# A two-layer transformer block on one Trainium2 core: output products that end tile by tile, a turned narrow product, index queries for three tiles, scores between transposes, and high parts made with one input

## What is computed

```python
# layer 1
y = concatenate([y_a, y_b, y_c]) * silu(z)
x = x + rms_norm(y @ w_out, post_norm_g)
# layer 2
h = rmsnorm(x, attn_norm)
q, k, v, iq, ik, iw, z, xbc, dt_raw, gate_a, gate_b = split(h @ w_in)
rel = relu(einsum('bqhd,bsd->bqhs', iq, ik) * IDX_DIM ** -0.5)      # 8 index heads of 64
score = einsum('bqhs,bqh->bqs', rel, iw * IDX_HEADS ** -0.5)
top_s, sel = top_k(where(admissible, score, -inf), 128)
o = softmax(q . k[sel]) @ v[sel]                                    # 16 heads, 4 of keys
merged = sigmoid(gate_a) * (o @ w_attn_branch) + sigmoid(gate_b) * (y_ssd @ w_ssd_branch)
x = x + merged @ w_out
x = x + hier_moe(rmsnorm(x, ffn_norm), ...)
```

## Time and profile before

| what | value |
|---|---|
| median of three runs | 1577.42 us (1576.61 to 1577.51) |
| the profiled execution, its own time | 1578.34 us |
| its span in the trace | 1576.5 us |
| PE busy | 1368.4 us (87%) |
| POOL busy | 827.3 us (52%) |
| DVE, ACT busy | 635.3 us, 378.2 us |
| mean granted clock of TensorE | 0.941 |

### The profile page before, as it was taken

One profiled execution on the slowest core, in us unless ns is written; L12 is line 12 of the kernel. 1 busy time (PEld: TensorE's weight loads), 2 busy tenths in 40 slices (PEclk: granted clock), 3 DMA queues, 4 the chain that ended last, 5 costly groups with the idle time before them and its releaser, 6 DMA issues.

```text
span 1576.5 us, 18167 instructions
## 1 busy us (share of the span) xinstructions
PE 1368.4 (87%) x7076; PEld 984.2 (62%) x7076; DVE 635.3 (40%) x929; ACT 378.2 (24%) x736; POOL 827.3 (52%) x712
## 2 busy tenths in 40 slices
PE   5898969589987978999999999968998499999993
PEld 5777747477766745678777878857877333333331
DVE  3131252324887056364877556463221411111112
ACT  3211053311130156311122544251003011111111
POOL 7678713537677710288888333749690213333320
PEclk9999989799999989999999999979997599999997
DMA  5423210132122210023222211352255079999964
GB/s 191 136 67 107 67 41 28 38 107 94 67 81 98 90 53 2 14 94 133 80 87 71 71 41 68 128 232 80 80 220 207 13 314 376 372 373 376 368 246 177
DMA packets 85237, 216.29 MB, mean 137 GB/s; under 512 B 23509, under 2 KB 32421, under 8 KB 71589
## 3 DMA queue, kind: packets, MB, share of 16 engines
q1 hardware_dynamic: 62076, 199.22, 33.7%
q0 software_dynamic: 13824, 8.44, 1.8%
q10 hardware_dynamic: 9256, 7.51, 1.5%
HBM read 255.99 MB, written 26.22 MB: 179 GB/s over the span
## 4 chain that ended last, share of the span: by engine, by line
PE 44%; issue 11%; POOL 11%; PEld 10%; DVE 9%; DMA 4%; DVEq 3%; ACT 3%; POOLq 3%; PEldq 2%; ACTq 1%; SPq 0%
PE ps L963 9%; PE ps L133 6%; PE ps L134 6%; PE ps L135 6%; POOL w_lo L487 6%; PE ps L975 5%; POOL w_hi L484 5%; PEld ps L133 4%; PEld ps L134 3%; PEld ps L135 3%; POOLq L485 2%; PE ps L734 2%; PE ps L955 2%; PE ps L822 1%; DMA w_gu<-w_up,over_u 1%
## 5 line engine op out<-in xcount | busy, mean ns | idle before, releaser
L484 POOL TENSOR_TENSOR w_hi<-stage,unit 128x512 fp32r<-128x512 f32 (+2 forms) x304 | 323.8, 1096 | 444.0 <-PE ps L135 434.3
L487 POOL TENSOR_TENSOR w_lo<-stage,w_hi 128x512 fp32r<-128x512 f32 (+2 forms) x304 | 404.7, 1362 | 10.8
L133 PE MATMUL ps<-hi,w_hi 128*128 128x512 f32 (+1 forms) x600 | 240.3, 401 | 31.8 <-POOL w_lo L487 17.9
L134 PE MATMUL ps<-hi,w_lo 128*128 128x512 f32 (+1 forms) x600 | 237.0, 395 | 0.0
L135 PE MATMUL ps<-lo,w_hi 128*128 128x512 f32 (+1 forms) x600 | 236.8, 395 | 0.0
L133 PE MATMUL ps<-w_hi,hi 128*128 128x512 f32 (+3 forms) x560 | 199.2, 356 | 12.6 <-POOL w_lo L487 6.6
L134 PE MATMUL ps<-w_hi,lo 128*128 128x512 f32 (+3 forms) x560 | 197.0, 352 | 0.0
L135 PE MATMUL ps<-w_lo,hi 128*128 128x512 f32 (+3 forms) x560 | 196.9, 352 | 0.0
L963 PE MATMUL ps<-w_gu,xT 128*64 128x512 f32 x768 | 172.0, 600 | 3.2 <-DMA w_gu<-w_up,over_u 1.8
L133 PEld LDWEIGHTS ps<-hi,w_hi 128*128 128x128 f32 x600 | 116.5, 194 | 63.1 <-issue 19.3
L135 PEld LDWEIGHTS ps<-lo,w_hi 128*128 128x128 f32 x600 | 116.4, 194 | 24.0
(11 more groups left out here) (393 smaller groups left out, 1714.7 us busy)
## 6 DMA issues: line engine op xcount, KB each, us to landing
stage<-w_in SPq DMA_DIRECT2D x84, 512.0 KB, 4.2
w_gu<-w_gate SPq DMA_DIRECT2D x32, 1024.0 KB, 11.6
w_gu<-w_up SPq DMA_DIRECT2D x32, 1024.0 KB, 13.7
...
```

What stands on the lines that cost most here:

```text
L133: pe.matmul(out, x[0], w[0], start=first, stop=False)
L134: pe.matmul(out, x[1], w[0], start=False, stop=False)
L484: nc.gpsimd.tensor_tensor(w_hi[:, b, k, 0:n], stage[:, b, k, 0:n], unit[:].broadcast_to([P, n]), ALU.mult)
L487: last = nc.gpsimd.tensor_tensor(w_lo[:, b, k, 0:n], stage[:, b, k, 0:n], w_hi[:, b, k, 0:n].bitcast(F32), ALU.subtract)
```

## The change

1. **High parts.** POOL makes `w_hi` with `tensor_scalar` times 1.0, not with `tensor_tensor` and a broadcast column of ones. Its loops are written out, and the clearing of `xg` also waits for the last use of the weights.
2. **Output products by tile.** Job 8's and job 37's product is `tokens_by_tile`: eight blocks of a tile and a half, in an order that ends tile 0 at the fourth block, tile 1 at the fifth, tile 2 at the seventh and tile 3 at the eighth. It waits for both halves of the weights ahead of its first matmul. The norm behind it goes by tile, and `turn_tiles` turns all eight chunks of a tile at once into both PSUM sets.
3. **Narrow product.** The 104-column job comes ahead of the index queries (in SP's loads and POOL's splits too), with the weights stationary: 24 matmuls of 512 columns, where 96 of 104 stood. ACT copies the result to `small`, and four transposes bring it back behind the index queries' product.
4. **Index path.** Product, rotation and transposes of the index queries are made for tiles 1 to 3. The scores of tile 1 put eight heads in one PSUM set.
5. **Attention.** The first scores are issued ahead of the loop, the scores of batch i+1 between the two halves of the transposes of batch i-1. Job 14's product moves into the second attention: four eighths, the first scores, four eighths. DVE waits `t_full` before it overwrites `pr`. `gate_next` is read out in step 0 of ACT's loop, from another buffer.

```diff
...
-halves(w2, 0, IQ2)
 for h in range(2):
     rows = slice(512 * h, 512 * (h + 1))
     a = w2[rows, IK2:IK2 + 72].rearrange("(k p) n -> p k n", p=P)
     b = w2[rows, DT2:DT2 + 32].rearrange("(k p) n -> p k n", p=P)
     tile(lambda t, a=a, b=b: [(t[:, :, 0:72], a), (t[:, :, 72:SMALL], b)])
+halves(w2, 0, IQ2)
 for c0 in (KV2, Q2, Q2 + 512, GA2, GB2, GA2 + 512, GB2 + 512, XBC2 + 2048):
...
     for k in range(HALF):
-        nc.gpsimd.tensor_tensor(w_hi[:, b, k, 0:n], stage[:, b, k, 0:n], unit[:].broadcast_to([P, n]), ALU.mult)
+        nc.gpsimd.tensor_scalar(w_hi[:, b, k, 0:n], stage[:, b, k, 0:n], 1.0, None, ALU.mult)
...
-split_job(JOB_SMALL, SMALL)
-with pool.Fori(JOB_SMALL + 1, JOB_Z) as i:
-    split_job(i)
-with pool.Fori(JOB_Z, JOB_Z + 4) as i:
-    split_job(i, 256)
-with pool.Fori(JOB_Z + 4, JOBS) as i:
-    split_job(i)
+narrow = {JOB_MQ: 256, JOB_SMALL: SMALL, **{JOB_Z + i: 256 for i in range(4)}}
+for i in range(1, JOBS):
+    split_job(i, narrow.get(i, 512))
...
+pool.wait_ge(w_used, 2 * JOBS)
...
+def tokens_by_tile():
+    s = turns.take()
+    both = (weights(), weights())
+    for t, half in ((0, 0), (1, 0), (2, 0), (0, 1), (1, 1), (3, 0), (2, 1), (3, 1)):
+        for k in range(HALF):
+            last = matmul3(pe, ps[s][:, t, :], parts(x_parts, everything, HALF * half + k, slice(P * t, P * (t + 1))),
+                           parts(w_parts, everything, both[half], k, slice(0, 512)),
+                           half == 0 and k == 0, half == 1 and k == HALF - 1)
+        if (t, half) == (3, 0):
+            last.then_inc(w_used, 1)
+        if half == 1:
+            last = pe.drain().then_inc(wo_tile, 1)
+            if t == 3:
+                pe.drain().then_inc(w_used, 1)
+    pe.drain().then_inc(turn_full, 1)
...
-    for c0 in (0, 4):
-        s = turns.take()
-        for t in range(TT):
-            pe.wait_ge(tile_rows, base + t + 1)
+    sets = (turns.take(), turns.take())
+    for t in range(TT):
+        pe.wait_ge(tile_rows, base + t + 1)
+        for c0, s in zip((0, 4), sets):
             for c in range(4):
                 last = pe.transpose(ps[s][:, c, P * t:P * (t + 1)], rows(t, c0 + c), ident[:])
-        last.then_inc(turn_full, 1)
+            if t == TT - 1:
+                last.then_inc(turn_full, 1)
...
+    chunks = first() if first else iter(())
+    for _ in range(4 if first else 0):
+        next(chunks)
     turns.settle(1)
+    scores(0, p_s).then_inc(s_full, 1)
+    for _ in chunks:
+        pass
     for i in range(batches + 2):
         if i == 1:
             turns.settle(0)
-        if i < batches:
-            if base + i > 0:
-                pe.wait_ge(s_free, base + i)
-            scores(i, p_s).then_inc(s_full, 1)
-        elif beside:
+        if i == 0:
+            pe.wait_ge(s_free, base + 1)
+            scores(1, p_s).then_inc(s_full, 1)
+        if i >= batches and beside:
             if i == batches:
...
                 if half == 0:
                     pe.wait_ge(exp_ready, base + b + 1)
+                elif i + 1 < batches:
+                    pe.wait_ge(s_free, base + i + 1)
+                    scores(i + 1, p_s).then_inc(s_full, 1)
                 if base + b + half > 0:
                     pe.wait_ge(pT_ready[1 - half], base + b + half)
...
 tokens(ready=6)
+tokens_by_tile()
+turn_tiles(lambda t, c: qt[:, t, P * c:P * (c + 1)], 0)
+s = turns.take()
+for half in range(2):
+    pe.wait_ge(lo_ready, 7 + half)
+    b = weights()
+    for k in range(HALF):
+        last = matmul3(pe, ps[s][0:SMALL, 0, :], parts(w_parts, everything, b, k, slice(0, SMALL)),
+                       parts(x_parts, everything, HALF * half + k, everything), half == 0 and k == 0, half == 1 and k == HALF - 1)
+    last.then_inc(w_used, 1)
+pe.drain().then_inc(turn_full, 1)
+tokens(tiles=range(1, TT))
+pe.wait_ge(small_turned, 1)
+s = turns.take()
+for t in range(TT):
+    last = pe.transpose(ps[s][:, t, 0:SMALL], small[:, P * t:P * (t + 1)], ident[0:SMALL, 0:SMALL])
+last.then_inc(turn_full, 1)
 tokens()
-turn_tiles(lambda t, c: qt[:, t, P * c:P * (c + 1)], 0)
-tokens(ready=8)
-tokens(n=SMALL)
-tokens()
 pe.wait_ge(iq_rows, 1)
-turn_rows(lambda t, c: iqt[:, t, P * c:P * (c + 1)], chunks=4)
+turn_rows(lambda t, c: iqt[:, t, P * c:P * (c + 1)], tiles=range(1, TT), chunks=4)
...
 for n in range(1, TT):
-    for h4 in range(2):
+    for h4 in range(1 if n == 1 else 2):
         s = turns.take()
-        for h in range(4):
+        for h in range(8 if n == 1 else 4):
...
-            last = pe.matmul(ps[s][:, h, 0:P * (n + 1)], iqT[lanes, i // 2, P * n:P * (n + 1)],
+            place = ps[s][:, 2 * (h % 2) + h // 4, 256 * (h // 2 % 2):256 * (h // 2 % 2 + 1)] if n == 1 else ps[s][:, h, 0:P * (n + 1)]
+            last = pe.matmul(place, iqT[lanes, i // 2, P * n:P * (n + 1)],
...
 turn_rows(lambda t, c: qt[:, t, P * c:P * (c + 1)])
-features()
...
+attention(16, scores2, values2, lambda b: query_block(b) + 1, lambda b: pr2[:, b % 2], lambda b: pT2, 8, feature_chunks, feature_chunks)
 pe.wait_ge(yah_ready, 16)
 pe.wait_ge(yal_ready, 16)
...
 tokens(ready=14)
-tokens()
+tokens_by_tile()
...
+    A.activation(qt[:, t, :], xres[:, t, :], ACT.Copy, scale=st[:, 2, 12 + t:13 + t]).then_inc(tile_rows, 1)
+for t in range(TT):
+    A.wait_ge(wo_tile, t + 1)
+    A.activation(yT[:, 0, :], ps[s][:, t, :], ACT.Square, accum_out=st[:, 0, 20 + t:21 + t])
+    A.drain().then_inc(wo_ready, 1)
+    A.wait_ge(ss_ready, t + 1)
+    A.activation(st[:, 1, 8 + t:9 + t], st[:, 0, 8 + t:9 + t], ACT.Sqrt, scale=1.0 / D, bias=st[:, 9, 0:1]).then_inc(post_root, 1)
+    if t > 0:
+        row_out(t - 1)
+    A.wait_ge(tile_ready, t + 1)
+    A.activation(junk, xres[:, t, :], ACT.Square, accum_out=st[:, 0, 12 + t:13 + t])
+    A.drain()
+    A.activation(st[:, 1, 12 + t:13 + t], st[:, 0, 12 + t:13 + t], ACT.Sqrt, scale=1.0 / D, bias=st[:, 9, 0:1]).then_inc(root_ready, 1)
+turns.skip()
+row_out(TT - 1)
 high_parts("attn")
 s = turns.see()
-A.activation(iqt[:], ps[s][:], ACT.Copy).then_inc(iq_ready, 1)
+A.activation(small[:], ps[s][0:SMALL, 0, :], ACT.Copy).then_inc(small_turned, 1)
+A.drain().then_inc(turn_free[s], 1)
+s = turns.see()
...
+A.activation(iqt[:, 1:TT], ps[s][:, 1:TT], ACT.Copy).then_inc(iq_ready, 1)
 A.drain().then_inc(turn_free[s], 1)
 s = turns.see()
...
         A.wait_ge(rel_used, i - 1)
-    A.activation(rel[i % 2][:, :, 0:P * (n + 1)], ps[s][:, :, 0:P * (n + 1)], ACT.Relu).then_inc(rel_ready, 1)
+    if i == 0:
+        A.activation(rel[0][:], ps[s][:], ACT.Relu).then_inc(rel_ready, 1)
+    else:
+        A.activation(rel[i % 2][:, :, 0:w], ps[s][:, :, 0:w], ACT.Relu).then_inc(rel_ready, 1)
     A.drain().then_inc(turn_free[s], 1)
-    if i in (1, 3):
+    if i in (0, 2):
         s = turns.see()
-        A.activation(qt[:, :, 256 * (i - 1):256 * (i - 1) + 512], ps[s][:], ACT.Copy).then_inc(q_ready, 1)
...
-A.drain().then_inc(turn_free[s], 1)
-A.dma_start(gates_dram[1], gate_next[:]).then_inc(gate_saved[1], 16)
 for i in range(16 + 2):
     if i < 16:
         softmax(i, 8, P * (query_block(i) + 1), pr2[:, i % 2], pr2[:, i % 2], False)
-    if i == 1:
-        A.wait_ge(gate_saved[1], 16)
+    if i == 0:
+        s = turns.see()
+        A.activation(gate_next[:], ps[s][:], ACT.Tanh, scale=0.5)
+        A.drain().then_inc(turn_free[s], 1)
+        A.dma_start(gates_dram[1], gate_next[:]).then_inc(gate_saved[1], 16)
     if 0 <= i - 1 < 16:
...
+            if i > 1:
+                V.wait_ge(t_full, 2 * i - 2)
...
-V.wait_ge(wo_ready, 2)
-s = turns.see()
-V.tensor_tensor(st[:, 0, 8:8 + TT], st[:, 0, 8:8 + TT], st[:, 0, 20:20 + TT], ALU.add).then_inc(ss_ready, 1)
-V.wait_ge(rms_ready, 4)
-V.reciprocal(st[:, 2, 8:8 + TT], st[:, 1, 8:8 + TT])
-V.drain()
+s = turns.next_set()
...
+    V.wait_ge(wo_ready, 2 + t)
+    V.tensor_tensor(st[:, 0, 8 + t:9 + t], st[:, 0, 8 + t:9 + t], st[:, 0, 20 + t:21 + t], ALU.add).then_inc(ss_ready, 1)
+    V.wait_ge(post_root, t + 1)
+    V.reciprocal(r, st[:, 1, 8 + t:9 + t])
+    V.drain()
     V.scalar_tensor_tensor(xn[:, t, 0:512], xn[:, t, 0:512], r, post_g[:, 0:512], ALU.mult, ALU.mult)
     V.scalar_tensor_tensor(xn[:, t, 512:D], ps[s][:, t, :], r, post_g[:, 512:D], ALU.mult, ALU.mult)
     V.drain()
     V.tensor_tensor(xres[:, t, :], xres[:, t, :], xn[:, t, :], ALU.add).then_inc(tile_ready, 1)
-    if t > 0:
-        recip(t - 1, 12, 0)
+    recip(t, 12, 0)
+turns.see()
 V.drain().then_inc(turn_free[s], 1)
-recip(TT - 1, 12, 0)
...
         V.wait_ge(s_full, 8 + i + 1)
+        if i > 1:
+            V.wait_ge(t_full, 2 * (8 + i) - 2)
         for h in range(4):
             V.tensor_tensor_reduce(pr2[:, i % 2, h, 0:width], p_s[:, h, 0:width], sel[:, n, 0:width],
...
-    if i == 1:
+    if i == 3:
         V.wait_ge(gate_saved[1], 16)
...
-s = turns.see()
+s = turns.next_set()
 for t in range(TT):
+    V.wait_ge(wo_tile, TT + t + 1)
     V.tensor_tensor(xres[:, t, 512:D], xres[:, t, 512:D], ps[s][:, t, :], ALU.add).then_inc(tile_ready, 1)
```

(10 more changed lines are left out.)

91 lines of the change are left out of this document (42 added, 49 removed).

## The result

| what | before | after |
|---|---|---|
| median | 1577.01 us (4 runs, 1575.06 to 1577.51) | 1589.05 us (4 runs, 1588.35 to 1589.79) |
| ratio to before | | 1.0079, 95% interval 1.0061 to 1.0096 |
| profiled execution, span | 1578.34, 1576.5 us | 1588.35, 1586.5 us |

The change makes the kernel 12 us slower. The forecast was 1536 with a range of 1515 to 1566: wrong, on the wrong side. It came out where rival (b) stands, to which I had given one chance in ten.

A forecast was written before the change was run, and what follows sets the result against it. PE, busy 87% of the span, was taken as the bound. The terms 18.7 + 6.5 - 4.3 + 7.9 + 0.75 - 2.8 + 18.9 - 4.2 = 41.5 us came off 1578.3, giving a median of 1536, range 1515 to 1566.

The forecast's parts named there:

- rival (b): POOL's splits: new high part slower than the low part's two-input form, gain gone from 1.27 us, 1590 at 1.43; chance 0.10.
- the price of the high part: POOL's time for one new high-part instruction, 0.74 to 0.76 us taken, between 0.47 and 1.01; old form 1.01.
- g: Time saved per half split on POOL: 1.0 us forecast, 2.1 at 0.47 us per high part, 0 at 1.01.
- First attention: First scores ahead of the loop, window batches' scores between transposes: 6.5 us gained, nothing in the memory batches.
- Layer 1's tail: Layer 1's output product by tile: 10.45 us lost by starting later, 6.1 gained behind it, net -4.3.
- Layer 2's tail: Output product at job 37 by tile: the same 10.45 us lost, 6.2 gained before routing, net -4.2.
- Narrow product and index queries: Fewer matmuls in both products and no wait ahead of keys and values, less new waits: net +7.9 us.
- Second attention: Scores between transposes and job 14's product around the first scores: +18.9 us, less 2.8 waiting for q's evacuation.
- The steady part: Second attention's steps: scores cover the wait for DVE's copy, 0.8 us in each of 12 batches with three widths, 9.6.
- The splits: PE's waits for POOL's half splits, from program start to behind `xtok`, shrink: 18.7 us gained at 1.0 us per half.
- the wait for both halves: Ahead of each output product's first matmul: start 8.3 us later, 1.65 for slower clock, some 0.5 for drains, 10.45 lost.
- Rival (d): Output products: waiting for both halves costs more than the tails return, 12.3 us more lost, 1549; chance 0.05.

The follow-up runs named there:

- e1: The changed kernel with the high part made by the old two-input broadcast form again; 1573.53 us, ratio 0.9961.
- e3: The changed kernel with the high part made by a converting copy; 1533.21 us, ratio 0.9721.
- e7: The kernel before with the high part made by a converting copy and POOL's loops written out; 1552.62 us, ratio 0.9871.
- e2: The kernel before with the one-input constant high part alone and POOL's loops written out; 1594.69 us, ratio 1.0103.
- e5: e3's kernel with the wait for the second half of the weights moved ahead of the fourth block in both output products; 1509.62 us, ratio 0.9595.
- e11: e5's kernel with both output products signalling their four tiles only after the last matmul; 1529.28 us, ratio 0.9691.
- e9: e5's kernel with job 14's product ahead of the second attention, as before the change; 1518.40 us, ratio 0.9622.
- e12: e5's kernel with the waits for turned keys and queries behind the first four eighths of job 14's product; 1507.90 us, ratio 0.9560.
- e6: e1's kernel with the wait for the second half of the weights moved ahead of the fourth block in both output products; 1549.42 us, ratio 0.9827.

## Why the prediction was wrong

**The step that failed is the price of the high part.** I bounded the new instruction by 0.47 us (from a clearing) and by 1.26 (the dearer of the old forms), took 0.75, and drew the sum from it. It measured 1.46, outside both ends, so g was -1.8 and not 1.0. The upper end had no reason that excluded more: rows 3 and 4 show no arithmetic with a constant on POOL, and "reads one input less" is not a duration. Rival (b) said that from 1.27 us on the gain is gone and that 1.43 gives 1590; the chip gave 1.46 and 1589. Its mechanism was right (a split as long as half a product, and longer waits ahead of jobs 8 and 37), its chance of 0.10 was too small for a price that no row showed. That its number fits to a microsecond is partly luck, as the next paragraph shows. The Trainium skill's figure (GPSIMD Engine Reference, § 3.1: 769 ns for 512 elements) agreed with my middle, and no form measured here has it.

**The price is not all of it.** Of the 53 us between 1536 and 1589, 36.5 are the price: 21 that the sum counted on for g = 1.0, and 15.5 that the dearer form costs (e1 to after). The other 16.5 are the order of the change, which is worth 4 us at g = 0 (e1) where the sum had 20. Rival (b) had both wrong, and they cancel: it went from 1557 up by 33 us, the chip from 1573.5 by 15.5.

**The price is not linear, as I had it.** I gave 20 us to every 0.25. From 0.57 to 1.01 (e3 to e1) it is 40 us, 23 to each 0.25; from 1.01 to 1.46 (e1 to after) 15.5 us, 8.6. By the ratios it is 38 and 19 us. In the old order the two steps are worth 23 us (e7) and 17 (e2). On the slow side something is given back, in what POOL does to DVE. The first taps of the convolution, POOL and DVE, in the kernel after:

```profile
782.64 6.32 POOL L489 TENSOR_SCALAR w_hi<-stage 128x512 fp32r<-128x512 f32 x4
783.86 2.92 DVE L1723 TENSOR_SCALAR xsT<-cpad,cols 128x512 f32<-128x512 f32 x4 [8.15 <-ACT cpad L1264]
```

In e3:

```profile
722.80 2.29 POOL L489 CAST w_hi<-stage 128x512 fp32r<-128x512 f32 x4 [1.76 <-PE ps L139]
725.24 5.58 POOL L492 TENSOR_TENSOR w_lo<-stage,w_hi 128x512 fp32r<-128x512 f32 x4
724.67 5.01 DVE L1723 TENSOR_SCALAR xsT<-cpad,cols 128x512 f32<-128x512 f32 x4 [8.54 <-ACT cpad L1264]
```

Such a tap takes 796 ns in the mean after, all of it beside the constant form. It takes 1233 in e1 and 1312 in e3, but there it lies mostly beside the two-input low part and not beside the high part. What each form does by itself is told by single taps of the second kind (`xsT<-cpad,cols,xsT`, L1727, L1730 in e1) that lie beside one form from start to end:

| POOL's form | its own time beside nothing | the tap beside it | run, start of the tap |
|---|---|---|---|
| none | | 0.74 us | e3, 731.96 |
| copy | 0.61 us | 1.09 us | e3, 735.79 |
| constant | 1.49 us | 1.09 us | after, 771.10 |
| two inputs, one broadcast | 1.04 us | 1.52 us | e1, 764.10 |
| two inputs | 1.26 us | 1.77 us | e3, 740.53 |

Over all such taps beside one form the means are 1.01 us (copy, e3), 0.92 (constant, after), 1.42 (broadcast, e1) and 1.67 (two inputs, e1). In the single taps of the table three forms hold a tap up by their own time less some 0.25 us. The constant form, the longest, holds it up by no more than the copy does. DVE is busy 40 us less after than before, and the convolution stage is no longer after (197.7 us) than in e1 (198.9), though POOL's halves are 1.8 us longer. That the shorter taps are what keeps the stage from growing is argued from these rows, not shown by a run. The rule of the Trainium skill that I cited (SBUF — State Buffer, "Who interferes with whom") speaks of who waits for whom by ports, and of an exclusive lock. A lock held for nearly all of POOL's instruction fits three of the forms, and not the constant form; that the form changes DVE's time this much the page does not say.

**Point by point, with the wrong price taken out** (e1 against before, where g = 0):

- First attention: forecast 6.5 gained, measured 7.2. Right; the memory batches keep a period of 4.7 us.
- Layer 1's tail: forecast at g = 0 a loss of 9.3 + 2.15, measured 9.1 + 3.3; forecast a gain of 6.1, measured 4.9 (6.6 after). The mechanism is right. What stands behind the wait was too small: the drains inside the product take 1.2 us (e5 against e11) and not 0.5, and the clock 2.1 (e1 against e5) and not the 1.65 that I took from shorter waits.
- Layer 2's tail: the same loss, measured 10.2 + 4.0 (the wait itself is 9.39); the gain of 6.2 was 4.9. But routing, which I had left out, took 3.0 us more. With the losses the term is -12.3 where I had -5.2, the largest miss but for the price.
- Narrow product and index queries: forecast 7.9 at g = 1, measured 4.0 at g = 0 and 6.5 at g = 1.75. The stall for the split ahead of the index queries was foreseen at 4 to 5 us; it is 8.2 after, 6.3 in e1 and 4.6 in e3. The narrow product was foreseen at 5.5 to 5.9 us and takes 8.50 in e1 and e3, with a clock of 0.50 for its first 3.75 us (e3). In e5, behind the same wait of 3.2 us, the clock is 1.00 and it takes 5.89; what makes that difference no run shows.
- Second attention: forecast 16.1, measured 12.2 in e1 and 14.3 in e3. The steady part was foreseen at 9.6 and is 9.6 (e9, with the first scores ahead of the loop in it). The start was foreseen at 9.3 - 2.8 = 6.5 and is 4.7. The wait for q's reading was 2.25 of the 2.8, and could be had back (e12).
- The splits: forecast 18.7 for g = 1.0. With the copy (g = 1.75, e1 to e3) start to attention gains 13.4 where I had 5.5 x 1.75 = 9.6, the convolution 9.1 where I had 9.6, and the stage to `xtok` 7.3 where I had 5.8. These three were short by some 5 us. Two others of the list failed: the wait ahead of job 13 fell only from 7.80 to 6.49 where I had 2.5 x 1.75 = 4.4, and the short waits behind `xtok` gave some 0.5 where I had 3.3 (the stage to job 37 is 2.3 us shorter, and 1.8 of it is the wait ahead of job 37). That the sum of the list comes out near its 18.7 x 1.75 = 32.7 (31.6 for these five) is luck in part.

**What I did not see as a choice** was the wait for both halves. I priced it at twice 10.45 and put it down as part of the bargain. e5 and e6 show that it buys nothing: without it the tails are no longer, and 20 to 24 us come back. The price was about right; that it need not be paid I did not see. Rival (d) named the wait with 12.3 us at stake; the chains did not queue up as it had it. But against the old high part the wait costs more than the dearer form does (24.1 us, e1 to e6, and 15.5).
